# Later mixer blocks of an encoder step: the first branch sum follows the scores, and VectorE reads the scores first

## The chip, the cores and the metric

One core of a Trainium2 chip runs the whole kernel in one launch. The metric is the device time of that launch in microseconds (us), taken over several runs. The core's engines run side by side, each through its own list of instructions, and meet at semaphores: TensorE (PE: matrix products and transposes, whose results land in the eight banks of PSUM), VectorE (DVE), ScalarE (ACT), GpSimd (POOL) and SyncE (SP). Most DMA is issued by SyncE. The row gathers, whose addresses are computed on the chip, are issued by GpSimd.

## The reference

One step of an encoder with one layer. 1024 prompt rows and 128 sample rows (8 streams of 16) of 1024 channels go through two mixers and an expert stage:

```python
h = rmsnorm(x); z = h @ w_in                    # 5888 columns: q, k, v of A; q, k, v, gate of B; branch gates
s = q @ k.T * 64**-0.5 - slopes * dist          # mixer A, 8 heads: own 64-chunk and the two before, float32
m = maximum(max(s), sink); p = exp(s - m); p /= sum(p) + exp(sink - m)
oa = p @ v
o = ((qb @ kb.T) * intra) @ vb + (qb @ state) * decay      # mixer B, retention, 4 heads, 128 x 256
ob = layernorm(o) * silu(rg)
mix = sigmoid(ga) * (oa @ w_branch_a) + sigmoid(gb) * (ob @ w_branch_b)
x = x + mix @ w_out
h2 = rmsnorm(x)                                  # then for each row: 8 heads x 16 best of 16384 experts
y = sum_k gate_k * gelu(h2 . expert_u[k]) * expert_v[k]    # 128 experts of a row
out = rmsnorm(x + y)
```

All is float32. The keys and values of the last window and the retention state are returned as well.

## The kernel before

The rows are worked in nine blocks of 128: block 0 holds the sample rows, blocks 1 to 8 the prompt. The program is a row of stages, each with its list for every engine:

- up to about 600 us: input projection of blocks 0 and 1, their mixers;
- to about 1190 us: the projection of blocks 2 to 8, while VectorE runs the experts of block 0 and the first 48 expert places of block 1;
- to about 1790 us: **the mixers of blocks 2 to 8**, and beside them the other 80 expert places of block 1; behind block 8, the queries and the search of block 2's experts. The change acts here (and on block 1's mixer, which uses the same functions);
- to the end: the experts of blocks 2 to 8 from a joint table `uv_d`, one gather of 1 MB for each of 896 places.

A block of the mixers runs through `pe_block`, `act_block` and `dve_block`. The work is skewed: in block n the engines do the attention and the retention of n, and between them (`merge`, from block 3 on) the branch sums, the merge, the output product and the residual of n - 1. In the order of the data:

1. TensorE transposes q, k of both mixers (L308). ScalarE and VectorE copy them out of PSUM (L669, L670; L698 to L702). TensorE computes the attention scores into banks 0 to 3 (L625), then the retention scores `pe_scores_b` into bank 4 (L347), then the transposes of block n - 1's gated retention rows (`pe_gated_transposes`, L315) into banks 6 and 7.
2. TensorE waits for `atm`, the retention scores times their decay mask, and then runs `pe_branches`: the first branch sum (L323, banks 4 and 5) and the second (L328, banks 6 and 7). The first had to wait because it writes bank 4, which VectorE reads for `atm`.
3. VectorE (`dve_block`): copies, the second norm of block n - 2 (`dve_norm2`), the swish gate of n - 1 (`dve_gate`, L432), the value copy and key decay (L708, L710), the biases (`dve_biases`, L436), expert work (`dve_point` 0), then the two reads of the scores (L722, L723), the mask product (L725), the maximum (`dve_softmax`, L392). ScalarE's eight exponentials (`act_exps`, L354) follow the maximum; `dve_probs` (L402, L404) follows them.
4. Then the probabilities' transposes (L639), the mix's transposes (L334, they wait for VectorE's merge L441, L443, L445), the attention output (L647), the retention output (L652, L653), the output product (L341), the state's update (L661, L746). `dve_retention_norm` (L413 to L425) reads the retention output, and the residual add (L450) the output product.

**The expert work** is given out as eight points per block, `dve_point(v, blk, j)`. An odd j is a group of three dots (L1496: a gathered row of `peer_u` times the token's row, summed), an even j a group of three accumulations (L1513: a gathered row of `peer_v` times its weight, added up in `AC`). The accumulations of a block use the weights from the dots of the block before. GpSimd fetches the rows by `pool_values` and `pool_dots`, in turns, three rows of 4 KB for each of the 128 tokens:

```python
if grp: g.wait_ge(d["accz"], BASE_V + grp * PG)        # pool_values: the three places of rv are used
if grp and grp * PG < REST: g.wait_ge(d["freed"], BASE_U + grp * PG)   # pool_dots: the same for ru
```

`rv` and `ru` have three places each (`PG` = 3), so a group's rows are asked for only when the group before is used up. There are 80 places: 27 groups of dots, of which the first 24 fall into blocks 2 to 7 and the last three (the last of them two rows) into block 8.

**SyncE** brings the rest, in the order of its own list: the block's projected rows (`z_d`, keys part behind `kdec`), four table copies of 512 KB behind them and, behind the transposes of the mix (`mixt`), the gates of the block (1.5 MB) and four table copies more. ScalarE copies the gated rows (`act_gated`, L369) into `yT`, whose place also holds the second norm's rows until they are stored.

## Time and profile before

| | us |
|---|---|
| time, median of 3 runs | 4076.27 (4074.62 to 4079.49) |
| profiled execution | 4112.39 |
| its span | 4110.5 |
| PE / DVE / ACT / POOL busy | 3301.0 / 2452.1 / 1096.7 / 1758.0 |
| granted TensorE clock, mean | 0.932 of full |

The share of busy time says little by itself, since the stages have different limits: from 1790 us on, for more than half of the time, the DMA engines move 410 to 420 GB/s and all waits lead to the expert rows. The mixer blocks stand ahead of that in the same serial program, and each is the same loop once more. So one looks at one loop: how long it is, how much of it each engine is busy, what each engine stands still for, and which of these waits is caused by another. In a timeline an instruction's start and the next one's start on the same engine tell how long it held the engine; `[idle before <- releaser]` tells how long the engine stood still ahead of it and whose work ended that.

### The profile page before, as it was taken

To read this page: it belongs to the slowest core of one execution; us is meant where nothing else is said; L and a number is where in the kernel's file an instruction comes from. 1 tells how busy PE (TensorE), PEld (TensorE's weight loads), DVE (VectorE), ACT (ScalarE), POOL (GpSimd) and SP (SyncE) were. 2 spreads that over 40 slices of the span, in tenths; PEclk is the share of its full clock that TensorE was granted. 3 is DMA by queue.
4 is the path that set the end of the run, shared out by engine and by line. 5 is a ranking of instruction groups with operands and counts; after the bars stand their busy time and mean duration, and the time that the engine had idled before them with its cause. 6 is when DMAs were issued, how large, how long until landed. Compare 5 with 4: busy or idle time off the path is not lost.

```text
span 4110.5 us, 32129 instructions
## 1 busy us (share of the span) xinstructions
PE 3301.0 (80%) x8957; PEld 1632.7 (40%) x8957; DVE 2452.1 (60%) x4977; ACT 1096.7 (27%) x2938; POOL 1758.0 (43%) x1588
## 2 busy tenths in 40 slices
PE   8775597999966888859779779878878978977776
PEld 5453254555644454424224224323333423422222
DVE  0122068995766777555854864774684585485444
ACT  2102010011113333223333233333333333333322
POOL 1020147774743333124454444444444444445553
PEclk9886897999987898979999999999999999999999
DMA  9898999998998888899999999999999999999998
GB/s 351 295 301 311 340 314 400 386 390 343 373 381 334 317 307 306 305 359 421 421 421 416 416 418 400 421 413 410 419 409 409 422 405 411 419 407 423 422 422 353
DMA packets 303298, 1560.95 MB, mean 380 GB/s; under 512 B 31248, under 2 KB 59152, under 8 KB 179856
## 3 DMA queue, kind: packets, MB, share of 16 engines
q0 software_dynamic: 228096, 1300.34, 79.3%
q1 hardware_dynamic: 60448, 237.77, 15.4%
q10 hardware_dynamic: 14592, 21.10, 1.4%
q8 instruction: 51, 0.84, 0.1%
q14 instruction: 111, 0.91, 0.1%
HBM read 1515.44 MB, written 179.04 MB: 412 GB/s over the span
## 4 chain that ended last, share of the span: by engine, by line
DMA 26%; PE 18%; issue 6%; DVE 4%; ACT 1%; POOL 1%; POOLq 0%; ACTq 0%; DVEq 0%
DMA ring<-uv_d,IXD_p 26%; PE ps L1838 15%; PE ps L1810 3%; DVE ring L1937 2%; ACT dg L1881 1%; POOL ring L2043 1%; ACT GE_p L1875 0%; DVE BP_p L1007 0%; DVE CA_p L1012 0%; DVE BV_p L1002 0%; PE ps L1827 0%; DVE CA_p L1419 0%; DVE DOT_p L1937 0%; DVE II_p L1359 0%; DVE ACC L1918 0%
## 5 line engine op out<-in xcount | busy, mean ns | idle before, releaser
L1838 PE MATMUL ps<-ring,dg 128*128 128x512 f32 x3584 | 1704.1, 614 | 456.5 <-ACT dg L1881 428.2
L2043 POOL DMA_INDIRECT ring<-uv_d,IXD_p x896 | 1081.3, 1207 | 1306.6 <-PE ps L1838 1050.1
L1937 DVE CUSTOM_DVE_ANT_0 ring<-ring,H 128x1024 f32<-128x1024 f32 x896 | 1094.6, 1224 | 888.5 <-DMA ring<-uv_d,IXD_p 866.0
L1838 PEld LDWEIGHTS ps<-ring,dg 128*128 128x128 f32 x3584 | 663.5, 194 | 1415.9 <-issue 717.7
L1260 PE MATMUL ps<-w,xg 128*128 128x368 f32 x1792 | 577.9, 482 | 43.8 <-issue 41.3
L1875 ACT ACTIVATE GE_p<-DOT_p 128x2 f32<-128x2 f32 x448 | 91.1, 203 | 1483.3 <-DVE DOT_p L1937 1483.3
L1260 PEld LDWEIGHTS ps<-w,xg 128*128 128x128 f32 x1792 | 345.6, 193 | 275.7 <-issue 70.2
L1881 ACT ACTIVATE dg<-gdi,GE_p 128x128 f32<-128x128 f32 x896 | 310.7, 394 | 48.3 <-ACT GE_p L1875 3.9
L1869 ACT ACTIVATE gdi<-ident,GD_p 128x128 f32<-128x128 f32 x896 | 303.2, 386 | 25.8 <-issue 19.4
L145 POOL DMA_DIRECT2D uv_d<-in_peer_u x88 | 45.7, 520 | 493.7 <-DMA uv_d<-in_peer_v 283.2
L1289 ACT ACTIVATE zo<-ps,rstd 128x368 f32<-128x368 f32 x112 | 62.6, 567 | 521.7 <-PE ps L1260 284.0
L1810 PE MATMUL ps<-rows,hT_p 128*128 128x512 f32 x384 | 197.0, 595 | 0.0
L1532 POOL DMA_INDIRECT rv<-in_peer_v,IXD x80 | 85.9, 1074 | 223.7 <-DVE AC L1513 207.2
L992 POOL DMA_INDIRECT rows<-in_peer_u,IXD_s x128 | 157.2, 1228 | 55.3 <-issue 43.0
L226 PE MATMUL ps<-w,xg 128*128 128x368 f32 x512 | 161.4, 479 | 13.9 <-DMA w<-in_w_in 13.9
L992 POOL DMA_INDIRECT rows<-in_peer_v,IXD_s x128 | 148.1, 1157 | 51.1 <-issue 38.1
L1124 DVE CUSTOM_DVE_ANT_0 rows<-rows,H_s 128x1024 f32<-128x1024 f32 x128 | 150.9, 1222 | 25.3 <-DMA rows<-in_peer_u,IXD_s 22.1
L1135 DVE SCALAR_TENSOR_TENSOR ACC_s<-rows,WG_s,ACC_s 128x1024 f32<-128x1024 f32 x126 | 155.5, 1293 | 9.4 <-issue 6.1
L1540 POOL DMA_INDIRECT ru<-in_peer_u,IXD x80 | 78.9, 986 | 133.7 <-DVE DOT L1496 95.0
L226 PEld LDWEIGHTS ps<-w,xg 128*128 128x128 f32 x512 | 98.7, 193 | 76.1 <-issue 16.4
L1513 DVE SCALAR_TENSOR_TENSOR AC<-rv,WG,AC 128x1024 f32<-128x1024 f32 x80 | 102.7, 1284 | 40.9 <-DMA rv<-in_peer_v,IXD 34.3
L1496 DVE CUSTOM_DVE_ANT_0 ru<-ru,H 128x1024 f32<-128x1024 f32 x80 | 95.9, 1222 | 38.2 <-DMA ru<-in_peer_u,IXD 34.6
(412 smaller groups left out, 2877.3 us busy)
## 6 DMA issues: line engine op xcount, KB each, us to landing
uv_d<-in_peer_u POOLq DMA_DIRECT2D x88, 512.0 KB, 5.2
uv_d<-in_peer_v POOLq DMA_DIRECT2D x88, 512.0 KB, 6.3
w<-in_w_in SPq DMA_DIRECT2D x8, 2944.0 KB
w<-in_w_in SPq DMA_DIRECT2D x16, 1472.0 KB
z_d<-zo ACTq DMA_DIRECT2D x16, 1288.0 KB
rows<-in_peer_w_q SPq DMA_DIRECT2D x20, 1024.0 KB
uv_d<-in_peer_u SPq DMA_DIRECT2D x40, 512.0 KB
uv_d<-in_peer_v SPq DMA_DIRECT2D x40, 512.0 KB
```

Of the source, the lines that this page charges most:

```text
L226: mm = T.matmul(ps[:, m % AB, 0:WC], xg0[:, k, b * P:(b + 1) * P], w0[:, p % 2, n % 2, k, :], start=(k == 0), stop=(k == KT - 1))
L992: gather = g.indirect_dma_start(ring[:, n % RING, :], None, t["peer_u"] if kind == "u" else t["peer_v"], bass.IndirectOffsetOnAxis(ap=inde ...
L1124: V.tensor_tensor_reduce(out=row, in0=row, in1=H2[:], scale=1.0, scalar=0.0, op0=ALU.mult, op1=ALU.add, accum_out=DOT[:, k:k + 1]).then_in ...
L1135: V.scalar_tensor_tensor(ACC[:, k % 2], row, WG[:, k:k + 1], ACC[:, k % 2], ALU.mult, ALU.add).then_inc(d["freed"], 1)
L1260: mm = T.matmul(ps[:, n % AB, 0:WC], xg[:, k, b * P:(b + 1) * P], w[:, tile % 2, k, :], start=(k == 0), stop=(k == KT - 1))
L1513: V.scalar_tensor_tensor(AC1[:], row, WG1[:, k % SET:k % SET + 1], AC1[:], ALU.mult, ALU.add).then_inc(d["accz"], 1)
L1810: mm = T.matmul(bank(2 + n), hT[:, k, :], wq[:, k, n * 512:(n + 1) * 512], start=(k == 0), stop=(k == KT - 1))
L1838: mm = T.matmul(bank(6 + n), dg[:, k % DR, :], ring[:, k % RS, D + n * 512:D + (n + 1) * 512], start=(k == 0), stop=(k == NK - 1))
L1869: S.activation(gdi[:, k % GR, :], ident[:], ACT.Copy, scale=GD[:, k:k + 1]).then_inc(e["gdi"], 1)
L1881: S.activation(dg[:, k % DR, :], gdi[:, k % GR, :], ACT.Copy, scale=GE[:, k:k + 1]).then_inc(e["diag"], 1)
L1937: V.tensor_tensor_reduce(out=row, in0=row, in1=H2[:], scale=1.0, scalar=0.0, op0=ALU.mult, op1=ALU.add, accum_out=DOT[:, k:k + 1]).then_in ...
L2043: g.indirect_dma_start(ring[:, n % RS, :], None, uv_d, bass.IndirectOffsetOnAxis(ap=IXD[:, n:n + 1], axis=0)).then_inc(s_ring[n % RS], 16)
```

## The change

The branch sums are split in two functions, the merge in two. In a block of the later mixers (and of block 1, without `merge`):

- TensorE: the first branch sum follows the attention scores at once, then the gated transposes. The retention scores come behind those, into bank 0 and no longer bank 4, and wait until VectorE has read the attention scores (`sm_s`). The second branch sum follows, then the waits for `atm` and `prob`.
- ScalarE: the exponentials come ahead of the copy of the gated rows.
- VectorE: the reads of the scores and the maximum come right behind the swish gate. The value copy, the key decay and the biases follow, then the mask product (from bank 0), the denominator, and only then the expert work: points 0 and 1, the first product of the merge, point 2, the rest of the merge, points 3 and 4, the retention norm, points 5 to 7.

TensorE, from the attention scores of a block to its probabilities' transposes (with the semaphore that each waits for), before:

```order
L625 MATMUL ps<-kaT,qaT_p 128x256 x7
L347 MATMUL ps<-qbT_p,kbT_p 128x128 [waits b_stn]
L347 MATMUL ps<-qbT_p,kbT_p 128x128 x3
L315 MATMUL ps<-ident,gates_p 128x128 [waits b_ysil]
L315 MATMUL ps<-ident,gates_p 128x128 x7
L323 MATMUL ps<-rows,oaT_p 128x512 [waits b_oatc,b_atm]
L323 MATMUL ps<-rows,oaT_p 128x512 x7
L328 MATMUL ps<-rows,yT_p 128x512 [waits b_ytc]
L328 MATMUL ps<-rows,yT_p 128x512 x15
L639 MATMUL ps<-ident,Pr_p 128x128 [waits b_prob]
```

and now:

```order
L632 MATMUL ps<-kaT,qaT_p 128x256 x7
L323 MATMUL ps<-rows,oaT_p 128x512 [waits b_oatc,b_stn]
L323 MATMUL ps<-rows,oaT_p 128x512 x7
L315 MATMUL ps<-ident,gates_p 128x128 [waits b_ysil]
L315 MATMUL ps<-ident,gates_p 128x128 x7
L350 MATMUL ps<-qbT_p,kbT_p 128x128 [waits b_sm_s]
L350 MATMUL ps<-qbT_p,kbT_p 128x128 x3
L331 MATMUL ps<-rows,yT_p 128x512 [waits b_ytc]
L331 MATMUL ps<-rows,yT_p 128x512 x15
L648 MATMUL ps<-ident,Pr_p 128x128 [waits b_prob,b_atm]
```

The product `ps<-rows,oaT_p` is the first branch sum, `ps<-rows,yT_p` the second, `ps<-ident,gates_p` the gated transposes, `ps<-qbT_p,kbT_p` the retention scores. The first branch sum moved ahead and lost its wait for `atm`; the retention scores moved behind it and gained one for `sm_s`.

VectorE, around the scores, the maximum and the biases (line numbers of the new file are up to 14 higher) (AC: accumulations, ru,DOT: dots, Pr_p: the scores), before:

```order
L710 TENSOR_SCALAR kdec_p<-rows,outd_p 128x128 x4
L436 TENSOR_TENSOR gates_p<-gates_p,bg_p 128x2048
L1504 TENSOR_TENSOR WG<-GE,GD 128x12
L1513 SCALAR_TENSOR_TENSOR AC<-rv,WG,AC 128x1024 x3
L722 SCALAR_TENSOR_TENSOR Pr_p<-ps,rows 128x8x128
L723 SCALAR_TENSOR_TENSOR Pr_p<-ps,rows 128x8x128
L725 TENSOR_TENSOR atm_p<-ps,intra_p 128x512
L392 TENSOR_REDUCE mx_p<-Pr_p 128x8
L394 TENSOR_TENSOR mx_p<-mx_p,sink_p 128x8
L396 TENSOR_SCALAR ngm_p<-mx_p 128x8
L397 TENSOR_TENSOR es_p<-sink_p,mx_p 128x8
```

and now:

```order
L720 SCALAR_TENSOR_TENSOR Pr_p<-ps,rows 128x8x128
L721 SCALAR_TENSOR_TENSOR Pr_p<-ps,rows 128x8x128
L395 TENSOR_REDUCE mx_p<-Pr_p 128x8
L397 TENSOR_TENSOR mx_p<-mx_p,sink_p 128x8
L399 TENSOR_SCALAR ngm_p<-mx_p 128x8
L400 TENSOR_TENSOR es_p<-sink_p,mx_p 128x8
L724 COPY va<-rows 128x128
L726 TENSOR_SCALAR kdec_p<-rows,outd_p 128x128 x4
L439 TENSOR_TENSOR gates_p<-gates_p,bg_p 128x2048
L733 TENSOR_TENSOR atm_p<-ps,intra_p 128x512
L405 TENSOR_TENSOR rs_p<-rs_p,es_p 128x8
L407 RECIPROCAL rs_p<-rs_p 128x8
```

Between the maximum and the denominator stood three dots, and three accumulations ahead of the scores; now the value copy, the key decay and the biases stand there, and the mask product behind them.

VectorE around the merge (gates_p: its three instructions), before:

```order
L1496 ISA DOT 128x1
L441 TENSOR_TENSOR gates_p<-gates_p,ps 128x1024
L443 TENSOR_TENSOR gates_p<-gates_p,ps 128x1024
L445 TENSOR_TENSOR gates_p<-gates_p 128x1024
L1513 SCALAR_TENSOR_TENSOR AC<-rv,WG,AC 128x1024 x3
L1496 ISA ru,DOT<-ru,H 128x1024
```

and now:

```order
L1507 ISA DOT 128x1
L444 TENSOR_TENSOR gates_p<-gates_p,ps 128x1024
L1524 SCALAR_TENSOR_TENSOR AC<-rv,WG,AC 128x1024 x3
L448 TENSOR_TENSOR gates_p<-gates_p,ps 128x1024
L450 TENSOR_TENSOR gates_p<-gates_p 128x1024
L1507 ISA ru,DOT<-ru,H 128x1024
```

Three accumulations moved in between the merge's first product and its second.

The diff, without the calls of the split functions elsewhere (block 0, block 1's tail, the last block's tail, where the two parts are called one after the other):

```diff
@@ -315,13 +315,16 @@
                     mm = T.transpose(ps[:, 6 + k // 4, (k % 4) * P:(k % 4 + 1) * P], z(RG + P * k, P), ident[:])
                 mm.then_inc(s["yt"], 1)
 
-            def pe_branches(pe, blk):
+            def pe_first_branch(pe, blk):
 
                 pe.wait_ge(s["oatc"], blk + 1)
                 for n in range(2):
                     for k in range(4):
                         mm = T.matmul(bank(4 + n), oaT[:, k, :], wa[:, k, n * 512:(n + 1) * 512], start=(k == 0), stop=(k == 3))
                 mm.then_inc(s["yb"], 1)
+
+            def pe_second_branch(pe, blk):
+
                 pe.wait_ge(s["ytc"], blk + 1)
                 for n in range(2):
                     for k in range(KT):
...
@@ -439,6 +442,8 @@
                 v.wait_ge(s["gates"], blk + 1)
                 v.wait_ge(s["yb"], blk + 1)
                 V.tensor_tensor(z(GA, D), z(GA, D), bank(4, 2), ALU.mult)
+
+            def dve_merge_rest(v, blk):
                 v.wait_ge(s["ya"], blk + 1)
                 V.tensor_tensor(z(GB, D), z(GB, D), bank(6, 2), ALU.mult).then_inc(s["mixb"], 1)
                 v.wait_ge(s["mixb"], blk + 1)
...
@@ -626,14 +633,16 @@
                                   kaT[HD * kv:HD * kv + HD, :, :].rearrange("p s n -> p (s n)"), start=True, stop=True)
             mm.then_inc(s["scores"], 1)
             pe.wait_ge(s["stn"], blk)
-            pe_scores_b(pe, blk, 4)
-            if merge:
-                pe_gated_transposes(pe, blk - 1)
-            pe.wait_ge(s["atm"], blk + 1)
             if merge:
                 if blk == 3:
                     pe.wait_ge(s_wb, 16 * 7)
-                pe_branches(pe, blk - 1)
+                pe_first_branch(pe, blk - 1)
+                pe_gated_transposes(pe, blk - 1)
+            pe.wait_ge(s["sm_s"], blk + 1)
+            pe_scores_b(pe, blk, 0)
+            if merge:
+                pe_second_branch(pe, blk - 1)
+            pe.wait_ge(s["atm"], blk + 1)
             pe.wait_ge(s["prob"], blk + 1)
             for n in range(2 * HA):
                 mm = T.transpose(ps[:, n // 4, (n % 4) * P:(n % 4 + 1) * P], Pr[:, n // 2, (n % 2) * P:(n % 2 + 1) * P], ident[:])
...
@@ -670,9 +679,9 @@
             S.activation(kbT[:].rearrange("p h n -> p (h n)"), bank(2), ACT.Copy).then_inc(s["qkv"], 1)
             if blk > 3:
                 act_root2(act, blk - 2)
+            act_exps(act, blk, 2 * P)
             if merge:
                 act_gated(act, blk - 1)
-            act_exps(act, blk, 2 * P)
             act.wait_ge(s["rden"], blk + 1)
             for h in range(HA):
                 e = S.activation(Pr[:, h], Pr[:, h], ACT.Copy, scale=rs[:, h:h + 1])
...
@@ -704,6 +713,13 @@
                 dve_norm2(v, blk - 2)
             if merge:
                 dve_gate(v, blk - 1)
+            if blk <= 2:
+                v.wait_ge(s_mask, 16 * 4 + 48 * blk)
+            v.wait_ge(s["scores"], blk + 1)
+            sc = ps[:, 0:4, :].rearrange("p b (h n) -> p (b h) n", h=2)
+            V.scalar_tensor_tensor(Pr[:, :, P:], sc[:, :, P:], HD ** -0.5, alibi[:, :, P:], ALU.mult, ALU.add)
+            V.scalar_tensor_tensor(Pr[:, :, 0:P], sc[:, :, 0:P], HD ** -0.5, alibi_c[:] if blk == 1 else alibi[:, :, 0:P], ALU.mult, ALU.add).then_inc(s["sm_s"], 1)
+            dve_softmax(v, blk, 2 * P, sink[:], step)
             wait_mixers(v, blk, half)
             step.did(V.tensor_copy(va[:, 1], z(VA, P, half)))
             for h in range(HB):
...
@@ -713,30 +729,23 @@
                 if blk == 3:
                     v.wait_ge(s_bw, 16 * 8)
                 dve_biases(v, blk - 1)
-
-            dve_point(v, blk, 0)
-            if blk <= 2:
-                v.wait_ge(s_mask, 16 * 4 + 48 * blk)
-            v.wait_ge(s["scores"], blk + 1)
-            sc = ps[:, 0:4, :].rearrange("p b (h n) -> p (b h) n", h=2)
-            V.scalar_tensor_tensor(Pr[:, :, P:], sc[:, :, P:], HD ** -0.5, alibi[:, :, P:], ALU.mult, ALU.add)
-            V.scalar_tensor_tensor(Pr[:, :, 0:P], sc[:, :, 0:P], HD ** -0.5, alibi_c[:] if blk == 1 else alibi[:, :, 0:P], ALU.mult, ALU.add).then_inc(s["sm_s"], 1)
             v.wait_ge(s["st"], blk + 1)
-            V.tensor_tensor(atm[:].rearrange("p h n -> p (h n)"), bank(4), intra[:].rearrange("p h n -> p (h n)"), ALU.mult).then_inc(s["atm"], 1)
-            dve_softmax(v, blk, 2 * P, sink[:], step)
-            dve_point(v, blk, 1)
+            V.tensor_tensor(atm[:].rearrange("p h n -> p (h n)"), bank(0), intra[:].rearrange("p h n -> p (h n)"), ALU.mult).then_inc(s["atm"], 1)
             dve_probs(v, blk, 2 * P, False)
-            for half_point in range(2, 4):
+            for half_point in range(2):
                 dve_point(v, blk, half_point)
             if merge:
                 dve_merge(v, blk - 1)
-            for half_point in range(4, 6):
+            dve_point(v, blk, 2)
+            if merge:
+                dve_merge_rest(v, blk - 1)
+            for half_point in range(3, 5):
                 dve_point(v, blk, half_point)
             v.wait_ge(s["oat"], blk + 1)
             V.tensor_copy(kaT[:, 0], kaT[:, 1])
             V.tensor_copy(va[:, 0], va[:, 1])
             dve_retention_norm(v, blk, 2, step)
-            for half_point in range(6, 8):
+            for half_point in range(5, 8):
                 dve_point(v, blk, half_point)
             if merge:
                 dve_residual(v, blk - 1)
...
```

## Rows read from the trace of the kernel before

**Rows 1.** busy us of PE, PEld, DVE, ACT, POOL by block; clock, DMA share, GB/s

```profile
1394.70:1463.20 68.50, 55.47 (x208) 32.09 (x207) 52.98 (x84) 25.43 (x45) 25.13 (x24) 0.93 0.86 312
...
1600.10:1667.10 67.00, 56.28 (x202) 32.86 (x201) 48.29 (x78) 25.42 (x45) 21.44 (x21) 0.87 0.74 272
1667.10:1790.00 122.90, 81.77 (x224) 40.88 (x222) 80.44 (x242) 23.06 (x27) 4.69 (x5) 0.81 0.93 322
```

**Rows 2.** who TensorE waited for, blocks 3 to 8: us, times, longest

```profile
PE ps L323 <- DVE atm_p L725: 38.4, 6, 9.1
```

**Rows 3.** TensorE's timeline, one block: start, us, engine, line, operation, [idle before]

```profile
1371.72 1.09 PE L334 MATMUL ps<-ident,gates_p 128*128 128x128 f32 x8 [0.83 <-DVE gates_p L445]
...
1379.74 13.90 PE L341 MATMUL ps<-wo_p,yT_p 128*128 128x512 f32 x32
...
1399.68 2.96 PE L625 MATMUL ps<-kaT,qaT_p 64*128 64x256 f32 x16 [2.90 <-ACT kbT_p L670]
...
1403.85 1.09 PE L315 MATMUL ps<-ident,gates_p 128*128 128x128 f32 x8
1414.02 9.71 PE L323 MATMUL ps<-rows,oaT_p 128*128 128x512 f32 x16 [9.07 <-DVE atm_p L725]
```

**Rows 4.** VectorE behind the second branch sum; the clock at the first's start (columns as rows 1)

```profile
1437.49 1.22 DVE L443 TENSOR_TENSOR gates_p<-gates_p,ps 128x1024 f32<-128x1024 f32 x1 [5.73 <-PE ps L328]
...
1411.00:1416.00 5.00, 1.99 (x3) 0.95 (x4) 5.00 (x5) 0.00 (x0) 2.82 (x3) 0.50 1.03 365
```

**Rows 5.** VectorE's timeline, the end of one block and the start of the next

```profile
1342.66 1.22 DVE L722 SCALAR_TENSOR_TENSOR Pr_p<-ps,rows 128x1024 f32<-128x1024 f32 x1
...
1345.52 2.28 DVE L392 TENSOR_REDUCE mx_p<-Pr_p 128x8 f32<-128x2048 f32 x1
...
1348.19 1.22 DVE L1496 CUSTOM_DVE_ANT_0 ru<-ru,H 128x1024 f32<-128x1024 f32 x1
...
1350.48 1.22 DVE L1496 CUSTOM_DVE_ANT_0 ru<-ru,H 128x1024 f32<-128x1024 f32 x1
...
1352.48 0.23 DVE L402 TENSOR_TENSOR rs_p<-rs_p,es_p 128x8 f32<-128x8 f32 x1 [0.77 <-ACT Pr_p L354]
...
1379.94 1.43 DVE L413 BATCH_NORM_STATS2 stats_p<-ps 128x6 f32<-128x256 f32 x4 [0.59 <-PE ps L653]
...
1382.46 1.90 DVE L425 TENSOR_SCALAR yn_p<-ps,mv_p,sdv_p 128x256 f32<-128x256 f32 x4
...
1394.73 1.22 DVE L450 TENSOR_TENSOR X_p<-X_p,ps 128x1024 f32<-128x1024 f32 x1
...
1403.71 0.22 DVE L708 COPY va<-rows 128x128 f32<-128x128 f32 x1
...
1407.04 4.06 DVE L1513 SCALAR_TENSOR_TENSOR AC<-rv,WG,AC 128x1024 f32<-128x1024 f32 x3
```

**Rows 6.** ScalarE's copy of the gated rows

```profile
1408.26 1.02 ACT L369 ACTIVATE yT_p<-ps 128x1024 f32<-128x1024 f32 x1 [7.12 <-DMA h_d<-yT_p]
```

**Rows 7.** row fetches with quiet DMA, and behind SyncE's burst

```profile
1352.52 0.94 POOL L1540 DMA_INDIRECT ru<-in_peer_u,IXD  x1 [5.55 <-DVE DOT L1496]
...
1355.39 1.09 POOL L1540 DMA_INDIRECT ru<-in_peer_u,IXD  x1 [0.30 <-issue]
...
1360.97 1.23 DVE L1496 CUSTOM_DVE_ANT_0 ru<-ru,H 128x1024 f32<-128x1024 f32 x1 [0.35 <-DMA ru<-in_peer_u,IXD]
...
1441.15 0.33 SPq L771 DMA_DIRECT2D gates_p<-z_d  x1
...
1444.76 1.14 POOL L1532 DMA_INDIRECT rv<-in_peer_v,IXD  x1 [9.88 <-DVE AC L1513]
...
1456.92 2.71 DVE L1513 SCALAR_TENSOR_TENSOR AC<-rv,WG,AC 128x1024 f32<-128x1024 f32 x2 [1.95 <-DMA rv<-in_peer_v,IXD]
```

**Rows 8.** VectorE's residual add of block 8

```profile
1667.06 1.22 DVE L450 TENSOR_TENSOR X_p<-X_p,ps 128x1024 f32<-128x1024 f32 x1 [5.33 <-PE ps L341]
```

**Rows 9.** busy time at the end of block 2

```profile
1253.00:1263.00 10.00, 3.04 (x13) 2.63 (x13) 5.97 (x17) 3.83 (x4) 5.30 (x6) 0.50 1.03 412
```

9 lines of the change are left out of this document (7 added, 2 removed).

## The prediction

> **What bounds the kernel now.** I read the busy time by stage first, then who waited for whom on TensorE and VectorE, then the timelines of one block. The change acts on the seven blocks of the late mixer stage, about 1200 to 1670 us. I count time from R, the start of the residual add L450; blocks repeat from R to R. One R is 1394.73, so the one before is about 1326.3. One block lasts 68.5 us, in which TensorE is busy 55.5, VectorE 53.0 and the DMA engines 0.86 of the time, so 59 us of work [rows 1]. Nobody is full; the block is a loop of waits. TensorE waits for the mask product atm before the first branch sum, 38.4 us over six blocks, 9.07 of them in the block shown [rows 2, 3]. VectorE waits for the second branch sum, 5.73 in the block shown [rows 4]. The two waits are one fact seen twice: TensorE stands idle early because VectorE does biases and three expert accumulations before it reads the scores, and VectorE pays it back later, behind TensorE's 23.4 us of branch sums (1414.02 to 1437.49). Two more things: the residual add at 1394.73 did not wait for TensorE (no idle in its row, while L341 started 13.9 us of work at 1379.74), so VectorE ends the block already, 1.1 us late [rows 3, 5]. And VectorE's expert work needs rows that GpSimd fetches three at a time into three places.
>
> **The change part by part**, for blocks 4 to 7, from R.
>
> *Start of the block, unchanged.* Scores start at R+4.95 and end at R+7.9; VectorE is through with the swish gate at R+9.0 (L708 follows it at 1403.71) [rows 3, 5].
>
> *VectorE reads the scores at once.* Two reads of 1.22, which overlap a little, are 2.3; the rest of the 2.9 from the first (1342.66) to the maximum (1345.52), 0.6, is the mask product. Maximum and three small ones: 2.7, until the dots start at 1348.19. So the maximum is through at R+14.0, and before at R+21.9. The eight exponentials let L402 start 4.3 us after that (1352.48): R+18.3, against R+26.2 [rows 5]. The moved work (value copy, key decay, biases: from 1403.71 to the first accumulation at 1407.04, 0.2 of that being the weight product, so 3.1 us) ends at R+17.1, beside the exponentials. That cover is whole: with it gone the work would cost its 3.1.
>
> *TensorE sums the first branch behind the scores.* It starts at R+7.9; L323 with 9.7 ran in part at a low clock, 0.50 granted from 1411 to 1416 behind the idle 9 us [rows 4]; at the full clock it would be half of L341, 7.0. The idle time, and with it the low clock, moves ahead of the scores now (L341 through by R+60, the next scores at R+71): they may take 5.7 in place of 3.0, and the sum 7.0. Either way it ends near R+17.6, and the maximum, up to 1.7 later, still has its exponentials done when the retention scores are. Gated transposes 1.1: R+18.6. Retention scores, for which I take 1.2 by the transposes' row, being as many columns for half the instructions: R+19.8. ScalarE's copy of the gated rows now stands behind the exponentials; it takes 1.02 and starts at R+18.7, its earlier wait for the store of h_d is past by then (it copied at 1408.26, R+13.5) [rows 3, 6]. So the second branch sum, as many instructions as L341 with its 13.9, runs R+20 to R+33.9, against R+42.8 before (L443 starts behind it at 1437.49, R+42.8) [rows 3, 4]. **TensorE gains 8.9 us.** From the mix TensorE needs 8.0 to L341 and 13.9 in it (1371.7 to 1379.74 to 1393.6).
>
> *VectorE behind it.* The mask product waits for the retention scores, R+19.8, and takes 0.6; the denominator 0.5: R+21.0. Now the expert work, three accumulations (4.1, row 1407.04) and three dots (3.45, three starts 1.15 apart by 1348.19 and 1350.48): R+28.6. Before, the same work, the denominator and the biases were through at R+26.6, the dots lying beside the exponentials. **So VectorE is 2 us later here than before**: it idles 2.7 us for the retention scores and has nothing to put beside the exponentials but the 3.1. All eight groups of expert work now lie behind the denominator; before, two lay ahead of it.
>
> *The price of a row fetch.* From the first of three fetches to the end of the third dot on them: 1352.52 to 1362.2, 9.6 us, with quiet DMA. With the burst that SyncE issues at the mix transposes (gates and table copies, 1441.15) it is 1444.76 to 1459.6, 14.9 us [rows 7]. GpSimd starts 0.9 after the last row of the group is used (third dot of the group 1350.48 and 1.15, GpSimd 1352.52) [rows 5, 7]. These are the bounds of what no row shows, the fetches at their new places:
> - second accumulations: fetched from R+26.0, quiet, done R+35.7. The branch was ready at R+33.9, so the merge is 1.8 us late; mix at R+38.1.
> - second dots: R+41.6.
> - third accumulations: fetched from R+36.5, three us ahead of the burst (mix transposes end R+39.3). Quiet R+46.3, in the burst R+51.5. I take R+47.6, since two of the three fetches go out ahead of it.
> - retention norm, now here: outputs ready R+46.1; 4.4 us and the two copies, 0.3 (1379.94 to 1384.36): R+52.3. Third dots 3.45: R+55.8.
> - fourth accumulations: R+59.9.
> - fourth dots: fetched only when the third are used, R+56.7, and then 9.6: **R+66.3**. TensorE's L341 is through at R+60.1.
>
> So a block takes 66.2 in place of 68.5: **-2.3 each**, five times (blocks 3 to 7; block 3 lacks the second norm before its scores, with the same terms behind them): -11.5. Bounds: third accumulations quiet and in the burst give R+64.8 and R+70.0, so -3.7 to +1.5 each.
>
> *Block 8* has two dots in group three, none in group four, and its residual waited 5.33 us for TensorE [rows 8]; it took 67.0. TensorE's bound is R+60.1; the weight chunks are loaded just when the second accumulations are fetched, so I take R+61.5: -5.5 (-7 to -3).
>
> *Block 2* has no merge. There the dots moved behind the denominator delay the first release of a row place: they started with the exponentials and now start behind the denominator, 4.3 + 0.5, less 0.6 for the mask product that now stands behind the maximum, so 4.2. Three more rounds of fetches follow. DMA is at 1.03 there, 412 GB/s [rows 9], so what is asked later finds a queue that is the same length: +2 (0 to +4.3). The early block 1 has no expert work; its maximum comes 0.6 earlier: nothing.
>
> *The stages behind.* The last search and the expert phase have their own chains; 122.9 us from the last R with DMA at 0.93 [rows 1], all triggered by events that move along. I let the shift pass whole.
>
> Sum: -11.5 - 5.5 + 2 = **-15.0**. The profiled execution took 4112.4 (span 4110.5), 36 above the median of the runs; the blocks' waits are the same in both, so I put the difference on the median: 4076.3 - 15.0 = **4061.3**.
>
> By the Trainium skill (DMA: Bandwidth & Descriptors, Anatomy of one DMA) a software-generated transfer costs 2.0 us and its bytes at 436 GB/s, so an estimate of 3.2 for 512 KB. The trace disagrees: the last of the quiet rows was issued at 1355.39 and awaited until 1360.97, 5.6. By the page's price each block would end some 2.4 sooner, an estimate near 4049. The measured price stands in the sum.
>
> **The rivals.**
> 1. *TensorE becomes the bound*: every fetch lands in time, the residual waits for L341 at R+60.1, as block 8 did. For it: TensorE's 8.9 us are real and block 8 shows the form. Against: fourth dots can't be fetched before the third are used, and 59 us of DMA work in 60 would leave no gap. Time: five times -8.4, -7, +2: 4029.
> 2. *The gain is given back whole by the fetches*: the third accumulations end at R+49.5, the block at R+68.2, and only block 8 gains. Time: -1.5 -5 +2, about 4072. For it: the burst rows, and VectorE 2 us later at R+28.6. Against: the burst begins after two of the three fetches.
> 3. *Slower*: the norm now stands between the second and third dots, with the serial chain norm, dots, release, fetch, dots behind it, 4.7+3.45+0.85+9.6 = 18.6 us. The block is slower than before from the point where the third accumulations end later than R+49.9. If they pay the full 14.9 and the last fetch half of the excess, 2.6, the block ends at R+72.6: five times +4.1, -3 and +2, about 4096. For it: DMA at 0.86 busy with 5 us bursts at 1.0. Against: the last fetch falls behind the burst, which has been served by about R+49.
>
> The Trainium skill (DMA: Bandwidth & Descriptors, SWDGE vs HWDGE vs iDMA) says each DMA engine takes its software-fed and hardware-fed queues in turn. By that rule a fetch in the burst pays double its transfer and never the whole burst ahead of it; the trace agrees in kind, 14.9 against 9.6. It speaks for the forecast and rival 2 over rival 3.
>
> **How the numbers follow.** Forecast 0.50 (4050 to 4068), rival 1 0.10, rival 2 0.24, rival 3 0.16. Under 0.2%, 8 us, no measurement of this kernel tells a change. Faster: 0.50 + 0.10 + 0.02 of rival 2 = 0.62. Slower: 0.13 of rival 3 (it begins at +0). Same: the rest, 0.25. Range: the forecast and rival 2 hold 0.74; reaching a little into both outer cases gives 4046 to 4082.
>
> **What would show it.** Right: no wait of TensorE for the mask product ahead of the first branch; the second branch done at about R+34; 2 to 3 us idle of VectorE before the mask product and again before the last dots, released by DMA; residual adds 65 to 67 apart; the last block near 61. Wrong: VectorE idle ahead of the residual for L341 in blocks 4 to 7 (rival 1); third accumulations ending beyond R+50 (rivals 2, 3); a later end of block 2 by more than 4; or a stage behind 1670 that doesn't keep its 123 us.

## The result: slower by 0.9%

| | before | after |
|---|---|---|
| time, median, the same chip (us) | 4075.52 (4 runs) | 4113.93 (4 runs, 4106.6 to 4118.28) |
| ratio | | 1.0091, 95% interval 1.0073 to 1.0108 |
| stage of blocks 2 to 8, from its first load of rows to the next stage's | 599.6 | 631.2 |
| first load to R of block 3 | 132.5 | 141.8 |
| R to R, blocks 4 to 7 | 68.3, 68.5, 68.8, 68.1 | 73.3, 73.8, 73.0, 72.7 |
| block 8 | 67.0 | 64.9 |
| last R to the next stage | 126.4 | 131.7 |

Forecast 4061.3, measured 4113.93: wrong in sign and out of the range. The spans of the two profiles (4110.5 and 4112.6) nearly agree, but only because the profiled execution of before lost time in the projection, ahead of this stage: its mixer stage starts at 1193.91, that of after at 1159.69, 34 us sooner, and from the projection's first load of weights on the mean granted clock was 0.94 there and 0.97 in after. So I compare the stage: +31.6 = 9.3 + 19.1 - 2.1 + 5.3. The last 5.3 is no finding, since this stretch lies between 124.3 and 132.3 in those kernels below that bring whole rows and leave the table copies in place, without an order in it. Of the 38.4 between the medians 6.8 stay unplaced.

I name the groups of expert work V0, D0, V1, D1, V2, D2, V3, D3: point 2n is the accumulations Vn, point 2n + 1 the dots Dn. SyncE's burst is the load of the gates (1.5 MB) and the four table copies (2 MB) that it issues behind the transposes of the mix.

The busy time of after by block (columns as in [rows 1]), one block, block 8 and the stretch behind:

```profile
1374.87:1448.70 73.83, 57.06 (x205) 33.60 (x205) 53.06 (x84) 25.44 (x45) 27.24 (x24) 0.87 0.82 287
1594.35:1659.22 64.87, 56.73 (x194) 33.83 (x195) 48.10 (x77) 25.45 (x45) 19.57 (x17) 0.87 0.73 257
1659.22:1781.00 121.78, 80.11 (x217) 38.97 (x214) 76.66 (x236) 20.42 (x23) 7.50 (x8) 0.82 0.94 327
```

Against [rows 1] TensorE and VectorE do the same work in 5.3 us more, and the DMA share is lower, 0.82. What VectorE waited for from 1215 to 1665 us, most of blocks 2 to 8 in both (total, times, longest), before:

```profile
DVE ru L1496 <- DMA ru<-in_peer_u,IXD: 34.6, 17, 8.3
DVE gates_p L443 <- PE ps L328: 32.0, 6, 5.8
DVE AC L1513 <- DMA rv<-in_peer_v,IXD: 13.4, 9, 2.3
```

and after:

```profile
DVE AC L1524 <- DMA rv<-in_peer_v,IXD: 56.7, 35, 5.9
DVE ru L1507 <- DMA ru<-in_peer_u,IXD: 26.9, 19, 5.5
DVE atm_p L733 <- PE ps L350: 15.5, 6, 3.3
...
DVE Pr_p L720 <- PE ps L632: 12.5, 6, 4.6
```

The wait of 32.0 for the second branch is gone, as meant. Waits for rows grew from 48.0 to 83.6, and 28.0 of new waits for TensorE stand at the head of the block. Since the stages of the two profiles lie 34 us apart, the same over blocks 4 to 7 alone: waits for rows 17.7 before and 48.4 after, nearly all of the growth in the accumulations (10.3 and 37.7). TensorE no longer waits for the mask product (38.4 in [rows 2]); it is served sooner and idles at the end of the block instead, ahead of the next scores, which start at R+5 in both kernels. Its longest waits of after (same stretch and columns):

```profile
PE ps L632 <- ACT kbT_p L679: 59.7, 5, 13.7
```

TensorE's timeline of the block whose R is 1374.87, against [rows 3]:

```profile
1379.82 5.65 PE L632 MATMUL ps<-kaT,qaT_p 64*128 64x256 f32 x16 [12.30 <-ACT kbT_p L679]
1385.40 9.09 PE L323 MATMUL ps<-rows,oaT_p 128*128 128x512 f32 x16
1394.32 1.04 PE L315 MATMUL ps<-ident,gates_p 128*128 128x128 f32 x8
...
1396.47 14.00 PE L331 MATMUL ps<-rows,yT_p 128*128 128x512 f32 x32 [0.22 <-ACT yT_p L372]
...
1415.06 1.09 PE L337 MATMUL ps<-ident,gates_p 128*128 128x128 f32 x8 [2.84 <-DVE gates_p L450]
```

VectorE's timeline of it, against [rows 5]:

```profile
1385.51 1.22 DVE L720 SCALAR_TENSOR_TENSOR Pr_p<-ps,rows 128x1024 f32<-128x1024 f32 x1 [1.58 <-PE ps L632]
...
1396.29 0.69 DVE L733 TENSOR_TENSOR atm_p<-ps,intra_p 128x512 f32<-128x512 f32 x1 [2.51 <-PE ps L350]
...
1397.53 4.07 DVE L1524 SCALAR_TENSOR_TENSOR AC<-rv,WG,AC 128x1024 f32<-128x1024 f32 x3
...
1411.33 1.28 DVE L1524 SCALAR_TENSOR_TENSOR AC<-rv,WG,AC 128x1024 f32<-128x1024 f32 x1 [0.21 <-DMA rv<-in_peer_v,IXD]
...
1418.46 1.28 DVE L1524 SCALAR_TENSOR_TENSOR AC<-rv,WG,AC 128x1024 f32<-128x1024 f32 x1
1425.61 1.28 DVE L1524 SCALAR_TENSOR_TENSOR AC<-rv,WG,AC 128x1024 f32<-128x1024 f32 x1 [5.87 <-DMA rv<-in_peer_v,IXD]
1428.14 1.28 DVE L1524 SCALAR_TENSOR_TENSOR AC<-rv,WG,AC 128x1024 f32<-128x1024 f32 x1 [1.24 <-DMA rv<-in_peer_v,IXD]
...
1436.41 1.22 DVE L1507 CUSTOM_DVE_ANT_0 ru<-ru,H 128x1024 f32<-128x1024 f32 x1
...
1447.55 1.23 DVE L1507 CUSTOM_DVE_ANT_0 ru<-ru,H 128x1024 f32<-128x1024 f32 x1 [0.81 <-DMA ru<-in_peer_u,IXD]
```

GpSimd's fetches in it, against [rows 7]:

```profile
1402.41 1.14 POOL L1543 DMA_INDIRECT rv<-in_peer_v,IXD  x1 [23.23 <-DVE AC L1524]
...
1413.42 0.94 POOL L1543 DMA_INDIRECT rv<-in_peer_v,IXD  x1 [1.49 <-DVE AC L1524]
...
1438.45 1.36 POOL L1551 DMA_INDIRECT ru<-in_peer_u,IXD  x1 [4.79 <-DVE DOT L1507]
```

and the first load of SyncE's burst:

```profile
1416.18 0.33 SPq L780 DMA_DIRECT2D gates_p<-z_d  x1
```

The reader is to see: for 23.23 us GpSimd has nothing to ask for, since all six places hold rows that VectorE has put off. Then it asks for nine rows of 512 KB from 1402.41 to 1416.12, and SyncE's burst comes 0.06 us behind the last. The rows of V2, asked for at R+38.5, are used up at R+54.5 (1429.4). Norm and D2 follow (R+62.8), then the rows of D3, asked for at R+63.6, are used up at the next R, R+73.8.

Which of V2's three rows are late matters for the cause. The first, asked for 2.76 us ahead of the gates load and right behind six other rows, was used without a wait (1418.46 above). In blocks 4 to 7 the time from issue to landing is 4.4 to 5.3 us for the first row, 9.6 to 10.9 for the second (1.52 ahead of the load) and 10.8 to 12.0 for the third (0.06 ahead). The six rows in front had all landed at R+41.5 in the block shown. What the two late rows shared the DMA engines with, from 1418.87 to 1422.87 (queue, packets, MB, share of the 16 engines; q1 is SyncE's, q0 GpSimd's):

```profile
q1 hardware_dynamic: 102, 1.25, 78.6%
q0 software_dynamic: 76, 0.30, 20.2%
```

and from 1427 to 1431, when the gates had landed and the table copies ran:

```profile
q1 hardware_dynamic: 225, 0.84, 51.0%
q0 software_dynamic: 224, 0.82, 50.8%
```

Beside the copies the two queues move the same bytes. Beside the gates load, whose packets are 12 KB (1.25 MB in 102) and those of the rows 4 KB, the rows get a fifth of the bytes.

The DMA share shows the stretch in which GpSimd asks for nothing. First before, R+12 to R+30 of the block from 1394.73:

```profile
1406.73:1424.73 18.00, 10.71 (x19) 4.66 (x20) 16.62 (x23) 9.82 (x28) 6.08 (x6) 0.72 0.90 335
```

and after, from R+12 to R+54:

```profile
1386.87:1404.87 18.00, 17.78 (x51) 8.64 (x50) 15.06 (x23) 11.66 (x28) 2.15 (x2) 0.93 0.60 203
1404.87:1416.87 12.00, 9.16 (x45) 5.60 (x44) 9.38 (x11) 2.62 (x3) 8.68 (x8) 1.00 0.88 290
1416.87:1428.87 12.00, 12.00 (x57) 8.11 (x56) 4.87 (x7) 2.22 (x3) 4.41 (x4) 1.00 0.96 369
```

TensorE is full where before it was not (17.78 against 10.71 of 18), and the DMA engines are the ones with a hole, 0.60 against 0.90. The loop traded an early hole on TensorE, which it made up for later in the block, for one on the transfers, which it did not.

### The profile page after: what moved, and what is told of

It reads as the page before. It is cut to its first block, busy times and chain, and to the rows that moved or that the text cites. A ratio compares the mean times of both kernels' runs of the same rounds, so it can differ in the third digit from the quotient of the medians.

```text
span 4112.6 us, 32142 instructions
## 1 busy us (share of the span) xinstructions
PE 3274.0 (80%) x8957; PEld 1630.8 (40%) x8957; DVE 2454.6 (60%) x4977; ACT 1095.9 (27%) x2938; POOL 1764.8 (43%) x1588
## 4 chain that ended last, share of the span: by engine, by line
DMA 25%; PE 18%; issue 7%; DVE 5%; ACT 1%; POOL 1%; POOLq 0%; ACTq 0%; DVEq 0%
DMA ring<-uv_d,IXD_p 25%; PE ps L1850 15%; PE ps L1822 3%; DVE ring L1949 2%; ACT dg L1893 1%; DVE BV_p L1013 1%; POOL ring L2055 1%; DVE BP_p L1018 0%; DVE CA_p L1023 0%; ACT GE_p L1887 0%; DVE CA_p L1430 0%; DVE DOT_p L1949 0%; DVE VV_p L1365 0%; DVE ACC L1930 0%; PE ps L1839 0%
## 5 line engine op out<-in xcount | busy, mean ns | idle before, releaser
L2055 POOL DMA_INDIRECT ring<-uv_d,IXD_p x896 | 1070.2, 1194 | 1324.3 <-PE ps L1850 1068.9
L1271 PE MATMUL ps<-w,xg 128*128 128x368 f32 x1792 | 554.3, 472 | 2.0 <-ACT SC_s L970 2.0
L1893 ACT ACTIVATE dg<-gdi,GE_p 128x128 f32<-128x128 f32 x896 | 310.7, 394 | 50.9 <-ACT GE_p L1887 3.9
L1881 ACT ACTIVATE gdi<-ident,GD_p 128x128 f32<-128x128 f32 x896 | 303.1, 386 | 26.1 <-issue 19.8
L1003 POOL DMA_INDIRECT rows<-in_peer_v,IXD_s x128 | 159.0, 1242 | 45.3 <-issue 38.1
L1135 DVE CUSTOM_DVE_ANT_0 rows<-rows,H_s 128x1024 f32<-128x1024 f32 x128 | 151.9, 1222 | 41.2 <-DMA rows<-in_peer_u,IXD_s 40.1
L226 PE MATMUL ps<-w,xg 128*128 128x368 f32 x512 | 160.1, 476 | 14.1 <-DMA w<-in_w_in 14.1
L1003 POOL DMA_INDIRECT rows<-in_peer_u,IXD_s x128 | 148.9, 1164 | 47.0 <-issue 38.9
L226 PEld LDWEIGHTS ps<-w,xg 128*128 128x128 f32 x512 | 98.0, 192 | 75.6 <-issue 15.4
```

The costliest lines, as they stand in the source:

```text
L226: mm = T.matmul(ps[:, m % AB, 0:WC], xg0[:, k, b * P:(b + 1) * P], w0[:, p % 2, n % 2, k, :], start=(k == 0), stop=(k == KT - 1))
L1003: gather = g.indirect_dma_start(ring[:, n % RING, :], None, t["peer_u"] if kind == "u" else t["peer_v"], bass.IndirectOffsetOnAxis(ap=inde ...
L1135: V.tensor_tensor_reduce(out=row, in0=row, in1=H2[:], scale=1.0, scalar=0.0, op0=ALU.mult, op1=ALU.add, accum_out=DOT[:, k:k + 1]).then_in ...
L1271: mm = T.matmul(ps[:, n % AB, 0:WC], xg[:, k, b * P:(b + 1) * P], w[:, tile % 2, k, :], start=(k == 0), stop=(k == KT - 1))
L1881: S.activation(gdi[:, k % GR, :], ident[:], ACT.Copy, scale=GD[:, k:k + 1]).then_inc(e["gdi"], 1)
L1893: S.activation(dg[:, k % DR, :], gdi[:, k % GR, :], ACT.Copy, scale=GE[:, k:k + 1]).then_inc(e["diag"], 1)
```

## The experiments

All of them, with what was seen in blocks 4 to 7 (block: mean of blocks 4 to 7; D1 and D2: mean end of the group in blocks 5 to 7, from R). Ratios are to runs of the kernel before on the same chip; the kernels ran on several chips, and what the kernel before takes differs among them. In the lists of orders the numbers 0 to 7 are the points, `merge` is the merge's first product, `rest` what is left of it.

| kernel | ratio [95%] | block | D1 ends | D2 ends |
|---|---|---|---|---|
| before | 1 | 68.4 | 36.1 | 52.5 |
| after | 1.0091 [1.0073, 1.0108] | 73.2 | 43.9 | 62.3 |
| 1 norm back | 1.0121 [1.0104, 1.0137] | 73.3 | 43.4 | 61.3 |
| 2 points early | 1.0032 [1.0020, 1.0045] | 69.3 | 41.3 | 55.2 |
| 3 after, short rows | 0.9944 [0.9924, 0.9964] | 64.4 | 42.0 | 56.9 |
| 4 before, short rows | 0.9951 [0.9936, 0.9967] | 67.1 | 34.1 | 52.4 |
| 5 TensorE alone | 0.9972 [0.9961, 0.9982] | 64.5 | 36.0 | 50.3 |
| 6 VectorE alone | 1.0105 [1.0090, 1.0121] | 75.0 | 48.6 | 63.5 |
| 7 no copies | 1.0209 [1.0190, 1.0227] | 71.8 | 43.4 | 61.0 |
| 8 early, merge whole | 1.0036 [1.0023, 1.0050] | 70.6 | 43.2 | 58.7 |
| 9 values first | 1.0110 [1.0078, 1.0142] | 72.7 | 44.0 | 62.4 |
| 10 early, values first | 1.0007 [0.9985, 1.0028] | 68.6 | 41.3 | 56.6 |
| 11 TensorE alone, V0 sooner | 0.9970 [0.9941, 0.9999] | 65.5 | 36.8 | 51.7 |
| 12 V0 ahead | 1.0031 [1.0005, 1.0057] | 71.9 | 45.0 | 60.5 |
| 13 V0, D0 ahead | 0.9957 [0.9931, 0.9983] | 65.7 | 34.9 | 49.9 |
| 14 TensorE alone again | 0.9939 [0.9905, 0.9973] | 64.7 | 36.3 | 53.2 |
| 15 merge later | 1.0100 [1.0062, 1.0138] | 74.9 | 41.8 | 63.9 |

### Which part of VectorE's order (1, 2)

The norm goes back between D2 and V3; or V0 and D0 go right behind the maximum.

```diff
 e1:  0 1 merge 2 rest 3 4 -norm 5 6 7        ->  0 1 merge 2 rest 3 4 5 norm 6 7
 e2:  max, values, biases, atm, probs, 0 1 ... ->  max, 0 1, values, biases, atm, probs, 2 merge 3 rest 4 5 norm 6 7
```

> The changed kernel with one thing undone: the retention norm stands again between the third dots and the fourth accumulations, as in the kernel before (points 3, 4, 5, norm, 6, 7). Theory A (the serial chain third accumulations, norm, third dots, release, fetch, fourth dots makes the block 73 us): the third accumulations still end near R+54.5, but the third dots end at R+58 and not R+62.6, and the last dots' rows are asked for 4.6 us earlier; residual adds 69 to 70 us apart, total 18 to 25 us under the changed kernel's 4114, so 4090 to 4096. Theory B (the fetches compete for the DMA engines, and the order on VectorE matters little): blocks stay at 72 to 74, total within 6 us of 4114.

Measured: 4115.99 beside 4070.45, blocks 73.3, as theory B said and not A. The norm's place is worth nothing: with it behind D2 the rows of D3 come sooner and are not the last thing any more, but V3 and the norm are.

> The changed kernel with the first accumulations and the first dots right behind the maximum, beside the exponentials and TensorE's first branch sum, ahead of the value copy, decay and biases; the norm stays between the second and third dots. Theory A (expert work starts 7 to 8 us too late in the block; the row places stand idle from R to R+21): all fetches start 7 us earlier, the third group before the burst of the gates and table copies; blocks of 62 to 66 us, total 30 to 50 under the changed kernel: 4065 to 4084, at or under the kernel before. Theory B (DMA engines bound the block with 59 us of work plus the contention): blocks no shorter than 68, total 4085 or more. Theory C, which blames the norm's place alone: the chain behind the norm is unchanged, blocks 70 or more.

Measured: 4085.43, blocks 69.3. By both numbers this is theory B's case (DMA engines bound the block), and theory A's 62 to 66 was missed; kernel 5 below, with blocks of 64.5 and the same rows to fetch, then rules B out. Moving two groups of 7.5 us gives back 3.9 us of the 4.8 lost in a block, and about two thirds of the total (1.0032 against 1.0091).

### The bytes of the rows (3, 4)

```diff
-g.indirect_dma_start(rv[:, k % PG, :], None, t["peer_v"],
+g.indirect_dma_start(rv[:, k % PG, 0:(64 if grp else D)], None, <the same table seen as rows of 64 numbers>,
```

The same is done to the rows of the dots. The two kernels leave out most of each row, and their dots multiply the token's row by itself, so what they return for the experts of block 1 is another number; the count of fetches, waits and instructions is that of the whole kernels.

> The changed kernel, but each fetch of the mixer stage's expert rows after the first group brings 64 numbers of a row and not 1024 (same count of fetches and waits; the dots multiply another tile, so the expert result of block 1 is another). It takes away 12 MB a block and keeps the round trip. Theory A (the fetched bytes, alone and in the burst, make the waits): residual adds 60 to 62 us apart, bound by TensorE, total about 60 to 80 under the changed kernel. Rival (the round trip of GpSimd and a DMA's fixed time make them): the waits of VectorE for rows stay over half of their 84 us, blocks 68 or more.

> The kernel before with the same short rows. There TensorE's loop with its wait for the mask product is nearly the bound (L341 is through 1.1 us before the residual add): blocks of 67 to 67.5 us in place of 68.4 by every theory, total within 15 us of the kernel before. The distance to the changed kernel with short rows is then what the new order is worth with the fetches out of the way: I expect 6 to 7 us a block.

Measured: 4046.69 and 4049.57, blocks 64.4 and 67.1. Blocks of 60 to 62, bound by TensorE, did not come, and the distance is 2.7 and not 6 to 7. Without the bytes the new order is worth 2.7 us a block, with them it costs 4.8. So rows cost the new order 8.8 a block and the old one 1.3. (Of the 12.6 us by which the stage of 3 is shorter than that of 4 only 2.9 arrive in the totals; where the rest goes is open.) And even here V2 was late; this is the longest total among VectorE's waits in the short-rows kernel of after (1215 to 1665 us):

```profile
DVE AC L1524 <- DMA rv<-in_peer_v,IXD: 28.2, 9, 4.8
```

Only one row of the three is late there, the third, asked for 0.01 to 0.06 us ahead of the gates load: it landed after 7.5 to 8.6 us in blocks 4 to 7, the second (1.3 to 1.6 ahead) after 2.5 to 2.8. So a small row too waits for SyncE's burst.

### One engine's part at a time (5, 6)

Kernel 5 has TensorE's list of after (retention scores in bank 0) and the other engines' of before, with the mask product behind the maximum. Kernel 6 has TensorE's list of before.

```diff
 e5, VectorE:  values, kdec, biases, 0, reads, max, atm, 1, probs, 2 3, merge, rest, 4 5, norm, 6 7
 e5, ScalarE:  gated copy, exponentials
 e6, TensorE:  scores, retention scores (bank 4), gated transposes, wait atm, first and second branch
```

> TensorE alone in the new order (first branch sum behind the scores, gated transposes, retention scores in bank 0 behind the reads of the scores, second branch sum); VectorE and ScalarE in the order of before: biases and point 0 ahead of the reads, mask product behind the maximum, point 1 beside the exponentials, points 2 and 3, the merge in one piece, 4, 5, norm, 6, 7. Theory A (the loss is VectorE's: all expert work behind the denominator leaves the row places full from R to R+27 and presses the fetches into the half with SyncE's bursts; TensorE's part of the change is a gain): residual adds of blocks 4 to 7 stand 63 to 66 apart against 68.2 before, 73.2 after; total 20 to 35 us under the kernel before. Rival B (the DMA engines bound a block whatever the order, and the order before is at their limit): 68 or more apart, total within 10 us of before. Rival C (the loss is TensorE's: cold clock at the scores and the late retention scores): 71 or more apart, total over before.

> VectorE and ScalarE in the new order; TensorE in the order of before, retention scores in bank 4 right behind the scores, both branch sums behind the mask product. Theory A (VectorE's order makes the loss): residual adds 71 to 76 apart, total 15 to 45 us over before. Rival C (the loss needs TensorE's new order): 66 to 69 apart, total at or under before.

Measured: 4063.23 beside 4075.35, blocks 64.5; and 4118.11, blocks 75.0. Theory A holds: TensorE's half is a gain of 3.9 us a block (12 us in all: the expected 20 to 35 was too much), VectorE's half alone makes more than the loss. From R+12 to R+54 of kernel 5 (R 1421.25):

```profile
1433.25:1451.25 18.00, 15.17 (x41) 7.78 (x41) 16.87 (x23) 10.36 (x28) 5.82 (x6) 0.81 0.91 339
1451.25:1463.25 12.00, 11.04 (x58) 6.95 (x58) 10.20 (x13) 5.56 (x5) 5.97 (x6) 1.00 0.89 300
1463.25:1475.25 12.00, 12.00 (x51) 7.60 (x47) 9.43 (x24) 4.43 (x5) 5.83 (x6) 1.00 1.00 398
```

No engine has the hole now: 0.91 against 0.60, and VectorE is busy 9.43 of 12 us in the last row, against 4.87 in after.

### The copies in the burst, and those behind kdec (7 to 10)

```diff
 e7:  -rest_of_table(sp, part, min(part + 2, TABLE_P))       (both places in the blocks)
      -rest_of_table(sp, TABLE_P, NEXP // P)   +rest_of_table(sp, TABLE_S, NEXP // P)     (behind them)
 e8:  as e2, but 2 merge rest 3 4 5
 e9:  after, with values and kdec ahead of the reads of the scores
 e10: e8 and e9
```

> The changed kernel with the table copies of these blocks (two times 2 MB in each block) moved behind the mixers; the later stage has them to do, some 28 MB at about 410 GB/s, so up to 70 us more there. Theory A1 (the third accumulations take 15.9 us because the burst of gates and copies stands in front of them): fetches fall to 10 to 12 us, waits of VectorE for rows fall to less than half, residual adds 66 to 70 apart against 73.2. Rival B1 (the fetch takes its time by itself, and the order of places alone makes the loss): the waits stay above 60 us over the blocks, adds over 72 apart.

> The changed kernel with points 0 and 1 right behind the maximum, then behind the denominator 2, the whole merge in one piece, 3, 4, 5, norm, 6, 7. The version with the second dots (3) between the merge's parts had residual adds 66 to 71 apart and VectorE 7.8 us waits of TensorE for the mix (L450). Theory A: the mix comes sooner, adds 65 to 68 apart, total within 10 us of before. Rival B (fetches bound the block, the merge's place is nothing): 68 to 70 apart, total 10 to 20 over before.

> The changed kernel with the value copy and the key decay ahead of the reads of the scores again, where VectorE waits 1.6 us anyway. SyncE's key load and its four copies behind kdec leave at R+10 and not at R+17, into time in which the DMA share was 0.33. Theory A (the loss is the place of the expert work; the copies are a small part, as the run without copies showed: 1.3 us a block): residual adds 71 to 73 apart against 73.2. Rival D (the late copies collide with the second accumulations' rows, and that is most of the loss): 69 or less, total 20 or more under the changed kernel.

> As the run with points 0 and 1 behind the maximum and the merge whole (residual adds 70.7 apart), with the value copy and the key decay ahead of the reads. There the copies left at R+24 to R+29, beside the rows of the second accumulations, whose waits were 1.4 and 3.3 us. Rival D, now together with the place of the expert work: both matter, and this order comes near to TensorE alone: 64 to 67 apart, total under before. Theory A alone: 69 to 70.5, total over before still.

Measured: 71.8, 70.6, 72.7, 68.6 (the 4164.7 of kernel 7 holds the copies in the later stage, so only its blocks count). Kernel 7 lies between its two theories, kernel 8 beyond both, kernel 9 in A's range, kernel 10 between its two. Without any copy V2 still came late:

```profile
1490.56 1.28 DVE L1524 SCALAR_TENSOR_TENSOR AC<-rv,WG,AC 128x1024 f32<-128x1024 f32 x1 [2.76 <-DMA rv<-in_peer_v,IXD]
1494.35 1.28 DVE L1524 SCALAR_TENSOR_TENSOR AC<-rv,WG,AC 128x1024 f32<-128x1024 f32 x1 [2.51 <-DMA rv<-in_peer_v,IXD]
```

It ended at R+52.9 there, at R+54.2 in after (means). Theory A1 (copies) is down to 1.4 us a block. The gates load is still there in kernel 7, and V2's rows beside it are as in after: the first landed after 4.6 to 5.2 us, the second after 7.9 to 11.5, the third after 10.1 to 11.3 (blocks 4 to 7). No kernel takes the gates load away; kernel 15 below moves it. Kernel 8's merge place gained nothing (70.6 against 69.3). The late kdec costs 0.5 in after, which is small beside the up to 3.5 us by which single blocks of one kernel differ between two profiles (5 and 14), and 2.1 beside V1 (8 against 10): rival D is a part of kernels 2 and 8, and no clear one of after.

### When the first place comes free (11 to 13), and 5 once more

```diff
 e11: e5 with 0 ahead of the biases
 e12: after with 0 ahead of the reads of the scores (then 1 merge 2 rest 3 4 norm 5 6 7)
 e13: values, kdec, 0, reads, max, 1, biases, atm, probs, 2 3 merge rest 4 5 norm 6 7
```

> TensorE alone in the new order, with point 0 ahead of the biases: its rows are used 2.2 us sooner and the next ones asked for at R+14.9 instead of R+17.2. In the block read of that kernel the DMA engines are at 1.02 from R+6 to R+24, so the rows sooner asked for land no sooner: I expect the same within 0.1% of TensorE alone, adds 63 to 65 apart. If the chain of places bounds (rows asked for sooner are used sooner): 1 to 2 us a block less, total 4050 to 4058.

> The changed kernel with one move: point 0 (three accumulations) stands between the swish gate and the reads of the scores. The first row place of a block is released at R+14 instead of R+28. Theory E (the release decides: over the kernels so far it stood at R+28, 25.6, 20.8, 17.2, 15.0 with residual adds 73.2, 75.0, 70.7, 64.5, 65.5 apart): 66 to 69 apart, total 15 to 30 us under the changed kernel. Rival F (mask product, biases and the split merge make the loss): over 71 apart, total within 10 us of the changed kernel.

> TensorE in the new order; VectorE: value copy, key decay, point 0, reads of the scores, maximum, point 1 beside the exponentials, then biases, mask product, denominator, points 2 and 3, the merge whole, 4, 5, norm, 6, 7. Against TensorE alone only the biases change place (from ahead of the reads to behind point 1), so the maximum comes 2.3 us sooner. With the DMA engines at 0.93 over such a block the bound is theirs: adds 62 to 65 apart, total within 0.1% of TensorE alone. If the maximum still matters: 61 to 62 apart, total 10 us or more under it.

> TensorE alone in the new order, measured once more: ratio to before 0.996 to 0.998 as the first time (0.9972), total 8 to 16 us under it.

Measured: 65.5, 71.9, 65.7, 64.7. Kernel 14's ratio of 0.9939 is beyond the 0.996 to 0.998 expected, though its interval reaches them. Theory E fell with kernel 12: GpSimd could ask at R+14.1, its longest stops up to the merge are 9.7 and 9.8 us in place of 23.2, and the block stayed at 71.9 (its total came down by more, to 1.0031; its stage is 619.0 us against 631.2 in after, which places half of that). In it VectorE ran dry in another way, at the merge:

```profile
1510.24 1.22 DVE L444 TENSOR_TENSOR gates_p<-gates_p,ps 128x1024 f32<-128x1024 f32 x1 [3.36 <-ACT gates_p L366]
...
1519.53 1.22 DVE L448 TENSOR_TENSOR gates_p<-gates_p,ps 128x1024 f32<-128x1024 f32 x1 [4.08 <-PE ps L331]
```

D1 stands behind the merge and ended at R+45. Rows asked for early help only if the next groups are also used early. Kernels 11 and 13 gained nothing over 5 by rows asked for or scores read sooner; the DMA share over blocks 4 to 7 is 0.90 in all three, which fits, but no run shows it as the reason.

### The last alternative: fetch ahead of the burst, merge later (15)

```diff
 e15: after with 0 1 2 3 merge rest 4 norm 5 6 7
```

> The changed kernel with the whole merge behind points 2 and 3, so the mix is ready some 4 us later (R+44.5 instead of R+40.2) and TensorE waits longer for it; the second dots end at R+41 instead of R+43.6, and the third accumulations and third dots are asked for (R+38.5, R+42) ahead of SyncE's burst, which the mix transposes release (R+45.5). Theory G (block end = serial fetches behind the second dots and the second accumulations, dearer when behind the burst): third accumulations end by R+50, the block takes 68 to 71 although TensorE is served later; total 10 to 30 us under the changed kernel. Rival H (the merge's time or TensorE's sets the block): 74 or more apart, total over the changed kernel.

Measured: 74.9, so rival H (its total, 1.0100 against 1.0091, says nothing by itself). The first half of theory G came as expected: V2, asked for ahead of the burst, ended at R+49.4, its last row nearly without a wait. GpSimd's fetch of V2 and SyncE's gates load, block with R 1449.92:

```profile
1488.38 1.19 POOL L1544 DMA_INDIRECT rv<-in_peer_v,IXD  x1 [1.86 <-DVE AC L1525]
...
1491.80 0.99 POOL L1544 DMA_INDIRECT rv<-in_peer_v,IXD  x1 [0.30 <-issue]
...
1497.56 0.33 SPq L781 DMA_DIRECT2D gates_p<-z_d  x1
```

The six rows of V1 and D1 are asked for just ahead of these three, as in after, but the load comes 5.8 us behind the last of them and not 0.06. From first issue to the end of use V2 then takes 11.1 us (1488.38 to 1499.5), against 15.9. So the load's place makes most of what V2 paid in after, and the six rows in front at most 1.5 over the quiet 9.6. But then VectorE waited for TensorE, whose mix was 5 us later (same block):

```profile
1498.24 1.28 DVE L1525 SCALAR_TENSOR_TENSOR AC<-rv,WG,AC 128x1024 f32<-128x1024 f32 x1 [0.16 <-DMA rv<-in_peer_v,IXD]
1503.32 0.23 DVE L745 COPY kaT<-kaT 128x128 f32<-128x128 f32 x1 [3.79 <-PE ps L656]
1506.23 1.42 DVE L416 BATCH_NORM_STATS2 stats_p<-ps 128x6 f32<-128x256 f32 x4 [2.43 <-PE ps L662]
```

D2 stood behind the norm and ended at R+63.9, and D3's fetch behind it again.

So the cause, read over all full-row kernels of the table: where D2 ends later than R+56 the block ends 10.4 to 12.0 us behind it (means) (after 10.9, kernel 6 11.5, 8 12.0, 12 11.4, 15 11.0): one more fetch of three rows in series. With short rows (3) it is 7.5. D2 was late for a different reason in each: V2's rows in after, its own rows in 8, 10 and 12, the norm in 15. What they share is that VectorE enters the second half of the block with too few groups done: D1 at R+41 to R+49, against R+36 before and in 5. That last step, groups done by the merge, is read from these kernels; no run changed it by itself with all else fixed, and it isn't enough alone: D1 ends at R+41.3 to R+41.8 in kernels 2, 10 and 15, and their blocks are 69.3, 68.6 and 74.9. What the runs show without it is that VectorE's order makes the loss (5 against after, 6 against before; ScalarE's two pieces of work changed places with it in both).

## Why the prediction was wrong

- **No wait ahead of the first branch: right.** The sizes were optimistic. With 12.30 idle ahead of them the scores took 5.65, which I had named but not carried on: VectorE waited 1.58 for them, and the maximum was through at R+15.7, not R+14.0. The first branch took 9.09, not 7.0, as the low clock lasted into it (granted 0.57 from 1385.40 to 1390.00; in kernel 5, where the scores stand behind 2.62 idle, the two take 2.96 and 7.13). Second branch R+35.4, not R+33.9: TensorE gained 7.4, not 8.9.
- **V0 and D0 done at R+28.6: R+30.1. V1 R+35.7: R+37.7. Mix R+38.1: R+40.1.** Right in kind, 2 late, all of it from the point above.
- **V2 done at R+47.6 (46.3 to 51.5): R+54.5.** This is the step that failed. Its fetch took 15.9 where I took 11.1, above even the 14.9 of the burst row, and began 2.1 later. I took a fetch's price as a property of the moment of its issue, quiet or in the burst [rows 7], and said that two of the three, issued ahead of the burst, would be nearly quiet. The lead was as forecast (first issue 2.76 us ahead of the burst), the price was not: only the first row was quiet (4.4 to 5.3 us to landing), the second, 1.52 ahead, took 9.6 to 10.9, the third 10.8 to 12.0. A row still on its way when the gates load starts shares the engines with it, and gets a fifth of the bytes. That nine fetches went out in 14 us (R+27.5 to R+41.3) keeps more of them on their way, but weighs less: with the same nine and the load 5.8 us later kernel 15 paid 11.1. V1's end to V2's end is 16.1 in after, 15.4 without the copies, 13.0 with short rows (means). (The quiet bound of R+46.3 should read R+46.1, 36.5 + 9.6, and the quiet fetch of [rows 7] is 9.7 by its rows; neither changes the sum.)
- **Norm, D2, V3: as said.** 4.6 and 3.5 behind V2. **D3 done at R+66.3: R+73.8.** The fetch took 10.2 for 9.6. So the block is 6.9 late by V2 (2.1 start, 4.8 price), 0.6 by D3.
- **All eight groups behind the denominator.** I wrote this down and priced it at 2 us of VectorE. It leaves GpSimd 23.23 us in which it can ask for nothing, and the fetches then come late, up to the gates load. The stop by itself isn't the price, since kernel 12 breaks it in two and still takes 71.9. From R to the denominator a block takes 22.3 now and 26.1 before (means of blocks 4 to 7), from the denominator to the next R 50.8 and 42.3: the early maximum gains 3.8 at the front, and 8.5 are lost behind it.
- **Block 2 +2, block 3 -2.3: together +9.3.** From one denominator to the next, block 2 to block 3, it is 64.6 against 64.3, so block 2 cost nothing; from block 3's denominator to R it is 50.9 against 41.6, which is all of it.
- **Block 8 -5.5: -2.1.** Few groups and a gain, the right side, R+64.9 and not R+61.5.
- **Rival 3** was this mechanism with its point (V2 later than R+49.9) and 0.16 of the chance; its price, 4.1 a block, came as 4.8. Its argument against, that the last fetch falls behind the burst, was true (10.2) and not needed.
## What to carry to other kernels

When an engine's other work is put behind a chain that is to run first, list what that work releases: here row places, which GpSimd can't fill for 23 us and then fills in one pack, up to the moment of a large load. Price a transfer at its new place by all that is on its way until it lands, what is issued just behind it included: 0.06 or 1.5 us of lead over a load of 1.5 MB didn't help, 5.8 us did. And try the two halves of such a change apart: TensorE's order alone is 0.28% and 0.61% under the kernel before in two measurements (0.9972 [0.9961, 0.9982], 0.9939 [0.9905, 0.9973]) and beats both kernels.

## What the runs showed of the hardware

- A group of three rows of 512 KB, from its first issue to the end of its use, takes 9.6 to 10.2 us alone, 11.1 behind six more rows with SyncE's burst 5.8 us behind the third (kernel 15), and 15.9 behind six more rows with the burst of 3.5 MB 0.06 us behind the third. Taking away the 2 MB of copies from the burst saved 0.7 (kernel 7).
- Where GpSimd's rows and SyncE's loads are on their way together, both queues move about as many packets, not as many bytes: 76 and 102 packets, 0.30 and 1.25 MB, beside the gates load; 224 and 225 packets, 0.82 and 0.84 MB, beside the table copies.
- The attention scores take 2.96 us behind an idle 2.90 and 5.65 behind 12.30, where the granted clock of the stretch is 0.50 (the lower level, 1.2 GHz):

```profile
1374.87:1386.87 12.00, 7.05 (x18) 5.02 (x19) 7.95 (x16) 6.39 (x9) 2.81 (x3) 0.50 0.94 324
```

- Of one program on one chip, the kernel before spread from 4070.04 to 4111.72 over 23 runs, on another from 4068.83 to 4079.0 over 13. So only ratios of one chip are used, and block lengths from the profiles (64.5 and 64.7 in the one kernel profiled twice, 5 and 14; single blocks of the two differ by up to 3.5 us).
